# A gate moved from VectorE's output blocks into GpSimd's pass over the output weights

## What is computed

```python
sh, sc, gt = adaln(c, w_ada[l], b_ada[l])
h_l = rmsnorm(x_l, norm_g[l]) * (1.0 + sc) + sh
u_l = h_l @ w_in[l]
...
out_l = mixer(u_l, keys_all, lp, rope, True)      # long convolution | attention | pooling
x_l = x_l + gt * (out_l @ w_out[l])
...
return rmsnorm(x_l, final_norm_g)
```

## Time and profile before

| what | value |
|---|---|
| median of 3 runs | 951.62 us (948.29 to 953.95) |
| the profiled execution, its own time | 948.54 us |
| its span in the trace | 946.7 us |
| granted TensorE clock, mean | 0.998 of full speed |
| TensorE busy | 920.8 us, 97% of the span |
| VectorE busy | 633.1 us, 67% |
| ScalarE busy | 397.8 us, 42% |
| GpSimd busy | 99.0 us, 10% |

### The profile page before, as it was taken

How to read it: one execution, slowest core, us unless ns; L and a number is a source line. 1 busy time by engine, 2 the same in 40 slices (tenths; PEclk the granted TensorE clock), 3 DMA queues, 4 the chain that set the end, 5 groups by cost and what they waited for, 6 DMA issues and landing times.

```text
span 946.7 us, 12282 instructions
## 1 busy us (share of the span) xinstructions
PE 920.8 (97%) x4890; PEld 763.1 (81%) x4890; DVE 633.1 (67%) x850; ACT 397.8 (42%) x622; POOL 99.0 (10%) x78
## 2 busy tenths in 40 slices
PE   5999999999999999999999999999999999999996
PEld 3666777888888888888888888889898888888885
DVE  2665889788967699656876754877776863414244
ACT  3555656545234443234133433654455451213124
POOL 1112200310003100000005530000000000202020
PEclk9999999999999999999999999999999999999999
DMA  9999932323223212277773251101000146223314
GB/s 367 419 422 377 348 141 88 100 90 99 80 89 100 68 67 80 77 258 272 284 281 132 89 184 61 56 12 56 12 29 28 45 158 243 89 89 102 119 47 178
DMA packets 29909, 138.11 MB, mean 146 GB/s; under 512 B 3899, under 2 KB 4347, under 8 KB 22812
## 3 DMA queue, kind: packets, MB, share of 16 engines
q1 hardware_dynamic: 29132, 136.67, 39.9%
q10 hardware_dynamic: 720, 0.65, 0.2%
HBM read 132.07 MB, written 4.19 MB: 144 GB/s over the span
## 4 chain that ended last, share of the span: by engine, by line
PE 86%; DVE 5%; DMA 3%; ACT 3%; issue 1%; POOLq 0%; SPq 0%; ACTq 0%; DVEq 0%
PE pp L1824 37%; PE pp L2134 18%; PE pp L1854 17%; PE pp L1771 4%; DMA wa_raw<-in_wa_dram 3%; PE pp L1748 2%; PE pp L2097 2%; PE pp L1775 1%; DMA ada_raw<-in_w_ada_dram 1%; PE pp L2089 1%; PE pp L2088 1%; DVE softmax_stats L1498 1%; DVE pt_lo L1513 1%; ACT U L885 1%; PE pp L1932 0%
## 5 line engine op out<-in xcount | busy, mean ns | idle before, releaser
L1824 PE MATMUL pp<-h_hi,w_hi 128*128 128x512 f32 x544 | 213.6, 393 | 0.8 <-ACT UG L682 0.6
L1824 PE MATMUL pp<-h_hi,w_lo 128*128 128x512 f32 x544 | 211.9, 389 | 0.0
L1824 PE MATMUL pp<-h_lo,w_hi 128*128 128x512 f32 x544 | 211.8, 389 | 0.0
L1203 DVE TENSOR_TENSOR w_lo<-w_raw,w_hi 128x1024 fp32r<-128x1024 f32 x68 | 87.8, 1291 | 79.9 <-ACT w_hi L678 79.7
L678 ACT ACTIVATE w_hi<-w_raw 128x1024 fp32r<-128x1024 f32 x68 | 71.9, 1058 | 152.5 <-PE pp L1824 104.9
L1824 PEld LDWEIGHTS pp<-h_hi,w_hi 128*128 128x128 f32 x544 | 102.2, 188 | 24.4 <-issue 1.9
L1824 PEld LDWEIGHTS pp<-h_hi,w_lo 128*128 128x128 f32 x544 | 102.1, 188 | 21.6
L1824 PEld LDWEIGHTS pp<-h_lo,w_hi 128*128 128x128 f32 x544 | 102.2, 188 | 20.6 <-issue 0.2
L2134 PE MATMUL pp<-wo_hi,m_hi 128*128 128x512 f32 x256 | 100.5, 393 | 0.0
L2134 PE MATMUL pp<-wo_hi,m_lo 128*128 128x512 f32 x256 | 99.6, 389 | 0.0
L2134 PE MATMUL pp<-wo_lo,m_hi 128*128 128x512 f32 x256 | 99.6, 389 | 0.0
(11 more groups left out here) (324 smaller groups left out, 1818.6 us busy)
## 6 DMA issues: line engine op xcount, KB each, us to landing
w_raw<-in_wb_dram SPq DMA_DIRECT2D x68, 512.0 KB, 3.6
ada_raw<-in_w_ada_dram SPq DMA_DIRECT2D x15, 2048.0 KB, 13.0
w_gate_raw<-in_w_gate_dram SPq DMA_DIRECT2D x16, 1024.0 KB, 4.9
wo_raw<-in_w_out_dram SPq DMA_DIRECT2D x16, 1024.0 KB, 4.8
wa_raw<-in_wa_dram SPq DMA_DIRECT2D x16, 320.0 KB, 7.8
UG<-in_xT_dram SPq DMA_DIRECT2D x8, 512.0 KB, 9.1
y<-in_x_dram SPq DMA_DIRECT2D x4, 1024.0 KB, 8.4
wh_raw<-in_w_heads_dram SPq DMA_DIRECT2D x4, 768.0 KB, 4.3
```

Source lines behind the costliest of these rows:

```text
L1203: eng.tensor_tensor(lane(wb_lo, n % KW), lane(wb_raw, n % KW), lane(wb_hi, n % 2), ALU.subtract).then_inc(wb_lo_done, 1)
L1824: mm = eng.matmul(ps[i][:], w, x, start=(kk == 0 and m == 0), stop=(kk == KT - 1 and m == 2))
```

## The change

GpSimd gets one more operation per chunk, `gated_weights(n)`: when chunk n has landed, it multiplies the raw weights in place by the gate's 512 columns of block b, repeated for the four k tiles by a stride of 0. ScalarE's high part waits for this product in place of the DMA. VectorE's product of the PSUM bank with the gate's row, and its wait, are left out of `residual`.

On GpSimd the products of chunks 0 to 7 stand ahead of everything of the output stage, those of chunks 8 to 11 behind the four gain products of block 0, and those of chunks 12 to 15 behind the gain products of block 1.

```diff
+            def gated_weights(n):
+
+                eng.wait_ge(wo_in[n % 3], 16 * (n // 3) + 16)
+                w = wo_raw[n % 3][:].rearrange("p (k c) -> p k c", k=4)
+                g = gate_rows_[:, (n // 4) * L:(n // 4 + 1) * L]
+                g = bass.AP(tensor=g.tensor, offset=g.offset, ap=[list(g.ap[0]), [0, 4], [1, L]])
+                eng.tensor_tensor(w, w, g, ALU.mult).then_inc(wo_gated, 1)
+
+            eng.wait_ge(gate_out, 1)
+            for n in range(8):
+                gated_weights(n)
 
             eng.wait_ge(gain_in, 16)
             for b in range(3):
+                if b:
+                    for n in range(4 * b + 4, 4 * b + 8):
+                        gated_weights(n)
                 for tok in range(4):
                     n = 4 * b + tok
                     eng.wait_ge(osq_done, n + 1)
...
             def wo_high(n):
-                eng.wait_ge(wo_in[n % 3], 16 * (n // 3) + 16)
+                eng.wait_ge(wo_gated, n + 1)
                 if n >= 2:
                     out_chunk_done(eng, n - 2)
...
                 bank = psum[:, 4 * (b % 2) + tok, :]
-                eng.tensor_tensor(bank, bank, gate_rows_[:, b * L:(b + 1) * L], ALU.mult).then_inc(oscaled, 1)
-                eng.wait_ge(oscaled, n + 1)
                 eng.tensor_tensor(yy, bank, yy, ALU.add).then_inc(res_done, 1)
```

More of the change, by code:

```diff
@@ L320, in backbone @@
         wo_hi, wo_lo, wo_mm, mm_done = sem("wo_hi_done"), sem("wo_lo_done"), sem("wo_mm"), sem("wo_bank_mm")
-        oscaled, res_done, osq_done, fin_done, stored = (sem("out_scaled"), sem("y_done_o"), sem("sq_done_o"),
+        wo_gated, res_done, osq_done, fin_done, stored = (sem("wo_gated"), sem("y_done_o"), sem("sq_done_o"),
                                                                      sem("fin_done"), sem("stored"))
```

## The result

The changed kernel takes 951.21 us (median of 20 runs), the kernel before 948.80 (median of 20; the 951.62 of the forecast was the median of the first three of them). The ratio is 1.0033, 95% interval 1.0017 to 1.0048: slower by about 0.3%, some 2.4 to 3 us, and within the 0.5% that was taken as no change. The 20 times lie between 950.46 and 959.05, those before between 948.15 and 955.61. The forecast step was +2.6 us, the range 949.4 to 958. The forecast time of 954.2 is 3 us too high because its base, the median of three runs, was.

The account below looks back on a forecast made before the run. TensorE was taken to bound the kernel, without a gap from 746 to 938.5 us. Terms 1.1 + 2.2 - 0.74 = +2.6 us on a median of 951.62 gave 954.2 us, range 949.4 to 958.

Parts of the forecast that it names:

- The sum: Whole kernel: 1.1 and 2.2 us lost in attention, 0.74 gained at the end, +2.6 us; chance 0.50.
- product 0: Chunk 0's GpSimd product, in attention: holds VectorE's rope subtraction 2.05 us, TensorE's wait at 727.5 grows by 1.1.
- product 1: Chunk 1's GpSimd product, in attention: keeps VectorE's softmax scaling at 746.74 out 2.9 us, TensorE waits 2.2.
- the gain alone: Rival: attention loses nothing to the GpSimd products, only the 0.74 us gain remains, time 950.9; chance 0.30.
- What bounds: From 746 us to 938.5, end of attention and output projection: TensorE has no gap, 192.50 of 192.50 us busy.
- One of the signs: Projection: ScalarE's high part still released by TensorE, one of the things said to show the forecast.
- The gain: Behind the last matmul: only the last token's VectorE product is on the path; removing it saves 0.74 us.
- Length of a product: GpSimd, 128x2048 by the repeated gate: 4.6 us, low bound 3.8, high bound 8.5.
- The lock: GpSimd keeps out VectorE operations with two SBUF inputs or in a fast mode; sum +2.6 with it, -0.7 without.
- Product 3: Chunk 3's GpSimd product, 776.3 to 780.9: VectorE's chunk 2 subtraction ends at 783.2, not 778.9; hidden by 2.6 us.
- the cover: Projection: 8.0 us of margin hides the products, gone if one takes over 12.6 us or, by GpSimd's queue, 9.6.
- long products: Rival: each further us of product costs 2 us in attention, over 0.5% from 5.7 us per product; chance 0.14.

Follow-up runs that it names:

- e3: Changed kernel with the GpSimd products of chunks 0 and 1 replaced by 8-column copies; 947.74 us, ratio to the kernel before 0.9973.
- e5: Changed kernel with only chunk 0's GpSimd product replaced by an 8-column copy; run once, span 947.8 us against the changed kernel's 949.2.
- e6: Changed kernel with only chunk 1's GpSimd product replaced by an 8-column copy; run once, span 946.8 us against the changed kernel's 949.2.
- e1: Changed kernel with GpSimd products for chunks 12 to 15 alone, VectorE's product kept in blocks 0 to 2; 947.74 us, ratio to the kernel before 0.9979.
- e2: Changed kernel with each GpSimd product cut into four instructions of 512 columns; 948.16 us, ratio to the kernel before 0.9985.
- e4: Changed kernel with VectorE's product and its wait kept in all 16 residuals; 951.82 us against the changed kernel's 951.21.
- e7: Changed kernel with each GpSimd product from chunk 4 on made twice; run once, span 977.0 us against the changed kernel's 949.2.
- e8: Changed kernel with each GpSimd product from chunk 4 on made three times; run once, span 1027.1 us against the changed kernel's 949.2.

## Why the prediction was right

- **The sum:** +2.6 us forecast, +2.4 in the medians and +2.5 in the spans. It is closer than its terms: 0.90 + 1.94 - 0.73 is 2.1, and 0.4 us that was not forecast (0.28 before product 0, 0.1 behind product 1) makes up the rest. That closeness is luck. The time alone would not have told the forecast from its rival: 951.21 lies below the 952 to 957 that the prediction gave as its likeliest, and 0.3 us from the 950.9 of the gain alone. It is the traces, and e3, e5 and e6, that decide for the forecast.
- **What bounds:** held. From 752.2 to 941.5 TensorE is busy 189.30 of 189.30 us, as in the earlier trace rows. One of the signs failed without harm: ScalarE's high part of chunk 4 was released by GpSimd's product and not by TensorE, with 5.2 us left in the end:

```profile
801.85 1.92 ACT L930 ACTIVATE wo_hi<-wo_raw 128x2048 fp32r<-128x2048 f32 x1 [10.22 <-POOL wo_raw L566]
```

- **The gain:** 0.74 forecast, 0.73 measured, and shown alone by e1.
- **Length of a product:** 4.6 forecast by taking the fixed 0.20 off three of four pieces, median 4.604. The repeated gate costs nothing that shows.
- **The lock:** shown for both kinds of VectorE operation. So the engines don't meet only at semaphores, as was said at the start: these two have no semaphore between them where they hold each other up. The row that was missing, the fast softmax scaling against a GpSimd product, reads 3.31 us in place of 0.62. The Trainium skill (SBUF — State Buffer, the section on who interferes with whom) has the lock as exclusive and held for the whole instruction, and e2 shows just that: cutting the instruction, with the work unchanged, shortens what VectorE loses to less than a piece, and the loss of TensorE is gone. (Only nearly: a part of 0.1 to 0.2 us ran inside the product, see product 1.) It was the right rule to give half of the chance to.
- **Product 0:** 1.1 forecast, 0.9 to 1.0 measured. The delay came out one wait earlier than I said: not at 727.5 but at 720.7, where TensorE's transposes wait for the pt_lo that stood behind the rope subtraction (they overwrite the PSUM that it reads). I had followed VectorE's queue to the next known wait and not asked which TensorE instruction waits for each delayed result.
- **Product 1:** 2.2 forecast, 1.9 measured. The product ended 2.9 us after the scaling's start, as forecast; the scaling was done 0.42 us later and not 0.62, so part of it had run inside the product's time (the same for the rope subtraction, 0.55 against 0.69). What the prediction didn't have is the stretch at the lower clock that followed this wait in e4 and e7, another 1.6 us in e4.
- **Product 3:** forecast as GpSimd first, VectorE waiting. It went the other way: VectorE's subtraction had begun 0.02 us earlier, and the product took 6.73. The product got in behind the subtraction, ahead of the m_lo queued there, and the first of those (782.01) ended at 787.11, before the end of chunk 1 near 789.7. Hidden either way.
- **The wrong number:** the cover. "Over 9.6 us" counted GpSimd's queue alone. By e7 and e8 VectorE's low part belongs to the same sum, with the 2 us that it holds GpSimd up: 10.88 - 1.3 - 2.0 = 7.6 us. That is an estimate from doubled and tripled products; no run has one product of such a length. The 12.6 us of the other bound is too high too: chunk 4 had 5.2 us in hand and not 8, which the prediction's own remark on that load (3 us later) would have given. The real product, 4.6, is below all of them, so nothing hung on it here. The chance given to long products rested on a threshold of 5.7 us from attention; since every product took about 4.6, no run tests it.

## What to carry to other kernels

Work moved to an idle GpSimd isn't free where VectorE is full, as this case shows: what counts is the length of one GpSimd instruction against the slack of the VectorE instructions with two SBUF inputs, or in the fast mode, that meet it. Cut it into pieces no longer than that slack (e2), or put it where VectorE idles (e1). And before moving all of a kind of work, ask which instance is on the path: here one of 16 products was, and moving only its block gave the gain without the loss. Last, a budget for GpSimd beside VectorE has to hold VectorE's two-input time as well as GpSimd's own: in e8 that was 2.0 us of 17.1 per chunk.

## What the runs showed of the hardware

- A GpSimd instruction keeps out VectorE's one-input 768-column scaling (0.62 us alone, 3.31 inside a 4.55 us product), and VectorE's operations on PSUM with one SBUF input pass beside it: the residual adds took 0.679 to 0.692 us in all 16 cases, both those of blocks 0 to 2, of which most ran inside a product (four from 815.63, product from 816.23 to 820.85), and the four of block 3, which met none.
- Where both engines had work queued, neither was shut out for longer than one instruction: in e2 four pieces of 1.29 us took 5.55 with VectorE's rope subtraction between the second and the third, and in e8 each low part of VectorE got in between two of the queued products and added 2.0 us to GpSimd's time.
- After the same wait of TensorE the granted clock can fall or stay: behind 1.86 us of waiting in e4 it was 0.50, the level of 1.2 GHz, for some 3 us, and behind 1.79 us in the changed kernel it stayed at 1.00. The fall cost e4 1.6 us. In e7's stretch from 860 to 970 us, in which TensorE waited again and again, the mean was 0.92.
